# Seven-product weight tiles taken one product after another, added up by TensorE on copies of its own sums, with every low part of these tiles on VectorE and six plain column tiles in place of four

## The chip, the cores and the metric

The kernel runs on one NeuronCore of a Trainium2 chip. The metric is the device time of one execution in microseconds (us), as the median of several runs.

## What is computed

A decoder trunk of two layers for 512 tokens of width 1024: layer 0 mixes with an RWKV-7 recurrence, layer 1 with dilated attention over keys and values that were made once from the stream. Each layer has a gated FFN (SwiGLU, width 2816) ahead of its mixer and one behind it, so four FFNs in all. The change touches the FFNs alone, and each of them computes

```python
def swiglu(h, w_in, w_out):
    gate, up = jnp.split(h @ w_in, 2, axis=-1)
    return (jax.nn.silu(gate) * up) @ w_out

x = x + 0.5 * swiglu(rms_norm(x, g), w_in, w_out)   # D_MODEL = 1024, D_FF = 2816, SEQ = 512
```

## The kernel before

The five engines run written-out programs of their own and meet at semaphores; nothing is scheduled by a library. Activations lie transposed, features on the partitions and the 512 tokens along the row. To keep float32 accuracy in TensorE's float32r format, each operand is split into a high part and a low part (the difference), and each product is made of three matmuls: high by high, high by low, low by high. The high part is a copy by ScalarE (ACT, `w_hi`), the low part a subtraction of two tiles in SBUF (`w_lo<-w_raw,w_hi`).

Weights come in chunks of 128 x 1024 values through four slots (`w_raw`, `w_hi`, `w_lo`, `SLOTS = 4`). A chunk's raw slot may be loaded again when its low part is made, its split parts may be overwritten when TensorE has used it (`w_used`).

An FFN has 22 column tiles of 128 hidden features (`FT`). They go through in three stages:

- **Plain groups.** `PLAIN = 2` groups of two column tiles each, four chunks to a group, 96 matmuls of 512 columns (gate and up, eight rows of 128 features, three products' parts). Group g uses banks 0 to 3 or 4 to 7. RMSNorm's factor `rstd` is multiplied in afterwards by VectorE (DVE), L747 and L749. GpSimd (POOL) makes the low parts, L343.
- **Seven-product tiles.** `TILES = 18` column tiles, two chunks each, from the normed stream `xa`. Gate and up of both halves of the tokens (256 each) over both halves of the features form a 2 x 2 by 2 x 2 block product, done with seven products instead of eight (Winograd's form of Strassen's). A product is 12 matmuls of 256 columns, a tile is 84. Before them VectorE makes sums of the weights, `weight_sums` (L588, L590, L591, L593; three into `wt`, one in place in `w_raw`), and once for each FFN the sums of the activations `xs`. The seven products of a tile lie in seven half banks, and each k-step issues a part of all seven. When the tile is done VectorE reads them and adds (L760 to L771: eight instructions of 128 x 256, each with one operand in PSUM), ScalarE takes Silu (L682), and VectorE multiplies to `hid` (L742). ScalarE makes the high parts (`weight_his`, L607 and L608); the low parts are divided: two sums and the chunk itself on GpSimd (L614, L343), the third sum on VectorE (L599).
- **Output rows.** 22 chunks of `w_out` by `hid`, 24 matmuls of 512 columns each, all eight banks.

Seven-product tiles alternate between banks 0 to 3 and 4 to 7. On each engine the order is that of the code: `step(n)` of VectorE, for instance, makes the weight sums of a later chunk, adds up tile n, makes the sums of the next chunk and its low part. `wt` and `wt_lo` share their memory, so the sums of a chunk also wait until TensorE has used the chunk four before it.

## Time and profile before

| | |
|---|---|
| median of 3 runs | 2620.65 us (2619.97 to 2623.49) |
| the profiled execution's own time | 2614.64 us |
| its span | 2612.9 us |
| TensorE busy | 2457.2 us, 94% of the span |
| VectorE busy | 1723.5 us, 66% |
| ScalarE busy | 1037.8 us, 40% |
| GpSimd busy | 1292.9 us, 49% |
| mean granted TensorE clock | 0.98 |

Busy time of TensorE (PE) is an upper bound of its work, since matmuls overlap: a 256-column matmul's record lasts 0.28 us, while the next one starts 0.12 us after it. So gaps and start-to-start times are read here, rather than busy shares. In rows of the trace, what stands in brackets is the time that the engine was idle before the instruction and what ended that idle time.

### The profile page before, as it was taken

The page shows a single profiled execution, that of the slowest core. Times are in us where ns is not written, and L with a number is a line of the kernel's source. Part 1 is how long each engine was busy: PE and PEld are TensorE (multiplying, and loading weights), DVE is VectorE, ACT ScalarE, POOL GpSimd, SP SyncE. Part 2 cuts the span into 40 slices and gives each one's busy share as a digit, 9 for nine tenths or more (in the row PEclk, how much of TensorE's full clock was granted, in tenths as well). Part 3 has the DMA queues.
Part 4 walks back from the last instruction along what each step waited for, and adds up shares of the span by engine and source line. Part 5 has one row for each costly group of instructions (what it writes and reads, how often), then busy time and mean ns, then how long its engine had stood idle before and what let it go on. Part 6 is the DMA issues. An engine that isn't in the chain of part 4 may idle for free.

```text
span 2612.9 us, 51432 instructions
## 1 busy us (share of the span) xinstructions
PE 2457.2 (94%) x20298; PEld 2110.5 (81%) x20298; DVE 1723.5 (66%) x2510; ACT 1037.8 (40%) x1655; POOL 1292.9 (49%) x641
## 2 busy tenths in 40 slices
PE   7899999998888989999999998999999998799998
PEld 6799886767776779988888878998888777699987
DVE  7999656456663799953433169995463566799943
ACT  4333324634562433332443233343353664333332
POOL 3777544333434467754344447775443102477742
PEclk9899999998998999999999999999999999899999
DMA  4233332210002223332344433333233241133331
GB/s 130 73 96 96 114 93 85 89 45 4 5 4 66 65 81 96 96 113 97 97 145 143 139 105 89 90 95 120 95 99 97 73 130 57 49 91 94 105 106 63
DMA packets 256570, 230.76 MB, mean 88 GB/s; under 512 B 17464, under 2 KB 194776, under 8 KB 256408
## 3 DMA queue, kind: packets, MB, share of 16 engines
q1 hardware_dynamic: 256408, 228.47, 28.1%
q8 instruction: 118, 1.93, 0.3%
q14 instruction: 44, 0.36, 0.0%
HBM read 213.73 MB, written 14.68 MB: 87 GB/s over the span
## 4 chain that ended last, share of the span: by engine, by line
PE 57%; POOL 18%; issue 16%; DVE 6%; ACT 2%; DMA 0%; POOLq 0%; SPq 0%; ACTq 0%; DVEq 0%
PE bank L368 9%; PE bank L370 9%; PE bank L369 9%; POOL wt_lo L614 8%; POOL w_lo L343 8%; PE bank L375 5%; PE bank L376 5%; PE bank L377 5%; DVE xa L621 2%; PE bank L2419 1%; PE bank L2406 1%; PE bank L2441 1%; POOL xs_lo L653 1%; PE bank L1635 1%; PE bank L1593 1%
## 5 line engine op out<-in xcount | busy, mean ns | idle before, releaser
L343 POOL TENSOR_TENSOR w_lo<-w_raw,w_hi 128x1024 fp32r<-128x1024 f32 x376 | 932.8, 2486 | 871.8 <-ACT w_hi L338 864.1
L338 ACT ACTIVATE w_hi<-w_raw 128x1024 fp32r<-128x1024 f32 x232 | 242.2, 1056 | 509.5 <-PE bank L370 336.0
L614 POOL TENSOR_TENSOR wt_lo<-wt,wt_hi 128x512 fp32r<-128x512 f32 x144 | 233.0, 1618 | 227.6 <-ACT w_hi L608 227.6
L883 PE MATMUL bank<-xa_hi,w_hi 128*128 128x256 f32 x864 | 258.9, 300 | 77.2 <-DVE wt_lo L599 38.2
L673 DVE TENSOR_TENSOR hid_hl<-hid,hid_hl 128x512 fp32r<-128x512 f32 x80 | 177.0, 2216 | 213.2 <-ACT hid_hl L667 213.2
L607 ACT ACTIVATE wt_hi<-wt 128x768 fp32r<-128x768 f32 x144 | 121.8, 846 | 466.4 <-DVE wt L593 465.7
L883 PEld LDWEIGHTS bank<-xa_hi,w_hi 128*128 128x128 f32 x864 | 166.5, 193 | 103.4 <-issue 85.9
L370 PE MATMUL bank<-hid_hl,w_lo 128*128 128x512 f32 x640 | 249.0, 389 | 0.0
L368 PE MATMUL bank<-hid_hl,w_hi 128*128 128x512 f32 x640 | 249.0, 389 | 0.0
L369 PE MATMUL bank<-hid_hl,w_hi 128*128 128x512 f32 x640 | 249.0, 389 | 0.0
L884 PE MATMUL bank<-xa_lo,w_hi 128*128 128x256 f32 x864 | 245.7, 284 | 0.0
L885 PE MATMUL bank<-xa_hi,w_lo 128*128 128x256 f32 x864 | 245.3, 284 | 0.0
L375 PE MATMUL bank<-w_hi,xg_hi 128*128 128x512 f32 x576 | 226.9, 394 | 0.0
L377 PE MATMUL bank<-w_lo,xg_hi 128*128 128x512 f32 x576 | 224.4, 390 | 0.0
L376 PE MATMUL bank<-w_hi,xg_lo 128*128 128x512 f32 x576 | 224.2, 389 | 0.0
L590 DVE TENSOR_TENSOR wt<-w_raw,wt 128x256 f32<-128x256 f32 x144 | 202.8, 1408 | 5.0
L884 PEld LDWEIGHTS bank<-xa_lo,w_hi 128*128 128x128 f32 x864 | 166.9, 193 | 0.2
L885 PEld LDWEIGHTS bank<-xa_hi,w_lo 128*128 128x128 f32 x864 | 166.7, 193 | 0.0
L883 PE MATMUL bank<-xs_hi,wt_hi 128*128 128x256 f32 x576 | 164.4, 286 | 0.0
L884 PE MATMUL bank<-xs_lo,wt_hi 128*128 128x256 f32 x576 | 164.4, 285 | 0.0
L885 PE MATMUL bank<-xs_hi,wt_lo 128*128 128x256 f32 x576 | 164.2, 285 | 0.0
L608 ACT ACTIVATE w_hi<-w_raw 128x1024 fp32r<-128x1024 f32 x144 | 150.3, 1044 | 0.0
(351 smaller groups left out, 6078.7 us busy)
## 6 DMA issues: line engine op xcount, KB each, us to landing
w_raw<-in_ffn_w_in SPq DMA_DIRECT2D x352, 256.0 KB, 3.2
w_raw<-in_ffn_w_out SPq DMA_DIRECT2D x176, 256.0 KB, 2.8
w_raw<-in_w_kv SPq DMA_DIRECT2D x96, 256.0 KB, 3.1
w_raw<-in_rwkv_w_rkv SPq DMA_DIRECT2D x48, 256.0 KB, 2.9
w_raw<-in_attn_w_q SPq DMA_DIRECT2D x48, 256.0 KB, 3.0
k_dram<-stage SPq DMA_DIRECT2D x6, 1024.0 KB, 4.6
v_dram<-stage SPq DMA_DIRECT2D x6, 1024.0 KB, 5.6
keys<-k_dram SPq DMA_DIRECT2D x24, 256.0 KB, 3.7
```

What stands on the lines that cost most here:

```text
L338: act.activation(w_hi[:, s, :], w_raw[:, s, :], ACT.Copy).then_inc(w_hi_ready, 1)
L343: pool.tensor_tensor(w_lo[:, s, :], w_raw[:, s, :], w_hi[:, s, :].bitcast(F32), ALU.subtract).then_inc(w_lo_ready, 1)
L368: pe.matmul(o, hi, x_hi, start=start, stop=False)
L369: pe.matmul(o, hi, x_lo, start=False, stop=False)
L370: return pe.matmul(o, lo, x_hi, start=False, stop=stop)
L375: pe.matmul(o, x_hi, hi, start=start, stop=False)
L376: pe.matmul(o, x_lo, hi, start=False, stop=False)
L377: return pe.matmul(o, x_hi, lo, start=False, stop=stop)
L614: pool.tensor_tensor(wt_lo[:, s, 0:2], wt[:, s, 0:2], wt_hi[:, s, 0:2].bitcast(F32), ALU.subtract)
L883: pe.matmul(o, hi, x_hi, start=k == 0 and m % 2 == 0, stop=False, skip_group_check=True)
L884: pe.matmul(o, hi, x_lo, start=False, stop=False, skip_group_check=True)
L885: last = pe.matmul(o, lo, x_hi, start=False, stop=k == KP - 1, skip_group_check=True)
```

## The change

- `PLAIN = 3`: three plain groups (six column tiles) and 16 seven-product tiles in each FFN.
- A tile's seven products are issued one after another, 12 matmuls each. Four half banks hold them: `C11`, `P5`, `C21`, `C12`. Where a product has to be added to several sums, ScalarE copies the running sum from one bank to the next (`copy` in `frame`), and TensorE adds its next product onto that copy. A tile has four such copies, counted by `snapshot`; TensorE waits for the first ahead of its third product, for the second ahead of its fifth, and for all four ahead of its last one. ScalarE takes Silu straight from the banks, in two halves. Of the eight additions of VectorE two remain (`ups`).
- All low parts of the seven-product stage are VectorE's: `weight_sums_lo` subtracts 128 x 768 and 128 x 1024; the seven `normed_los` are VectorE's too. GpSimd does nothing in this stage. Two counters of chunks take the place of one (`wait_lo`).
- In the plain stage ScalarE's order changes: all four chunks 4 to 7 are split before Silu and before the high parts of the normed stream.

```diff
-        PLAIN = 2
+        PLAIN = 3
...
-        def weight_last_lo(dve, ph, q, i=None):
+        def weight_sums_lo(dve, ph, q, i=None):
...
             dve.wait_ge(w_hi_ready, plus(c + 1, i, SLOTS))
-            dve.tensor_tensor(wt_lo[:, s, 2], wt[:, s, 2], wt_hi[:, s, 2].bitcast(F32), ALU.subtract).then_inc(wt_last_ready, 1)
+            dve.tensor_tensor(wt_lo[:, s], wt[:, s], wt_hi[:, s].bitcast(F32), ALU.subtract)
+            dve.tensor_tensor(w_lo[:, s, :], w_raw[:, s, :], w_hi[:, s, :].bitcast(F32), ALU.subtract).then_inc(wt_lo_ready, 1)
...
-        def weight_los(pool, ph, q, i=None):
-            c = seven_start(ph) + q
-            s = c % SLOTS
-            pool.wait_ge(w_hi_ready, plus(c + 1, i, SLOTS))
-            pool.tensor_tensor(wt_lo[:, s, 0:2], wt[:, s, 0:2], wt_hi[:, s, 0:2].bitcast(F32), ALU.subtract)
-            split_lo(pool, c, i, SLOTS)
...
+            def copy(n, product, dst, src, i=None):
+                act.wait_ge(product_done, plus(5 * (ph["nth"] * TILES + n) + product, i, 10))
+                act.activation(dst, src, ACT.Copy).then_inc(snapshot, 1)
...
+            def frame(n, i=None):
+                his(2 * n + 2, i)
+                copy(n, P1_DONE, seven_bank(n, C21), seven_bank(n, C11), i)
...
+                    second_silu(n - 1, i)
+                his(2 * n + 3, i)
+                copy(n, P6_DONE, seven_bank(n, C12), seven_bank(n, C21), i)
+                copy(n, P5_DONE, part[:, n % 2, 0], seven_bank(n, P5), i)
+                copy(n, P7_DONE, part[:, n % 2, 1], seven_bank(n, C21), i)
...
+                act.activation(gate[:, n % 2, first], seven_bank(n, C11), ACT.Silu)
...
-            for j in range(SLOTS, 2 * SLOTS - 1):
-                split_hi(act, c0 + j)
-            normed_his(act, ph, slice(0, 4))
-            split_hi(act, c0 + 2 * SLOTS - 1)
-            for t in range(2):
-                silu(t)
-            normed_his(act, ph, slice(4, 7))
+            for j in range(SLOTS, 2 * SLOTS):
+                split_hi(act, c0 + j)
+            for t in range(2):
+                silu(t)
+            for j in range(2 * SLOTS, 2 * SLOTS + 2):
+                split_hi(act, c0 + j)
...
+            normed_his(act, ph, slice(0, 3))
+            split_hi(act, c0 + 2 * SLOTS + 2)
+            normed_his(act, ph, slice(3, 7))
+            split_hi(act, c0 + 2 * SLOTS + 3)
...
-            if ph["update"] is None:
-                for i in range(2):
-                    dve.wait_ge(stored[i], 16 * (len(KV_GROUPS) // 2))
             normed_dve(dve, ph)
-            plain(0)
-            weight_sums(dve, ph, 0)
-            normed_lo_dve(dve, ph)
-            weight_last_lo(dve, ph, 0)
+            plain_scaled(0)
+            normed_los(dve, ph, slice(A11, S2))
+            plain_times(0)
+            normed_los(dve, ph, slice(S2, S3))
+            plain_scaled(1)
+            plain_times(1)
+            weight_sums(dve, ph, 0)
             weight_sums(dve, ph, 1)
+            for q in range(2):
+                weight_sums_lo(dve, ph, q)
+            normed_los(dve, ph, slice(S3, A22 + 1))
             weight_sums(dve, ph, 2)
...
+                product(n, c11, b11, A11, start=True).then_inc(product_done, 1)
+                product(n, p5, t1, S1, start=True).then_inc(product_done, 1)
+                read(1)
+                product(n, c21, t2, S2).then_inc(product_done, 1)
+                product(n, c11, b21, A12).then_inc(product_done, 1)
+                read(2)
+                product(n, c21, t3, S3).then_inc(product_done, 1)
+                product(n, c12, b22, S4, js=(0,))
+                read(4)
+                product(n, c21, t4, A22, js=(0,)).then_inc(w_used, 1)
+                product(n, c12, b22, S4, js=(1,))
+                product(n, c21, t4, A22, js=(1,)).then_inc(w_used, 1)
```

On ScalarE, a steady seven-product tile of the first FFN stood so before (in brackets the semaphores that a row waits for; L607 and L608 are the high parts of a chunk's sums and of the chunk, L682 is Silu):

```order
L607 ACTIVATE wt_hi<-wt 128x768 [waits w_used,wt_ready]
L608 ACTIVATE w_hi<-w_raw 128x1024
L607 ACTIVATE wt_hi<-wt 128x768 [waits w_used,wt_ready]
L608 ACTIVATE w_hi<-w_raw 128x1024
L682 ACTIVATE gate<-gate 128x512 [waits gate_scaled]
```

and stands so now (L706 are the copies of sums, L710 and L726 the two halves of Silu):

```order
L631 ACTIVATE wt_hi<-wt 128x768 [waits w_used,wt_ready]
L632 ACTIVATE w_hi<-w_raw 128x1024
L706 ACTIVATE bank<-bank 128x256 [waits product_done]
L710 ACTIVATE gate<-bank 128x256 [waits w_used]
L631 ACTIVATE wt_hi<-wt 128x768 [waits w_used,wt_ready]
L632 ACTIVATE w_hi<-w_raw 128x1024
L706 ACTIVATE bank<-bank 128x256 [waits product_done]
L706 ACTIVATE part<-bank 128x256 [waits product_done] x2
L726 ACTIVATE gate<-bank 128x256
```

ScalarE's row of a tile has gained four copies and one Silu instruction, and the first copy stands behind the high parts of the next tile's first chunk.

On VectorE, the same tile stood so before (L588 to L593 are the weight sums, L599 a low part, L760 to L771 the additions):

```order
L588 TENSOR_TENSOR wt<-w_raw 128x256 [waits w_used,w_landed1_1,w_landed1_0]
L590 TENSOR_TENSOR wt<-w_raw,wt 128x256 [waits wt_step]
L591 TENSOR_TENSOR w_raw<-w_raw 128x2x128
L593 TENSOR_TENSOR wt<-w_raw,wt 128x256 [waits wt_step]
L599 TENSOR_TENSOR wt_lo<-wt,wt_hi 128x256 [waits w_hi_ready]
L760 COPY part<-bank 128x256 [waits w_used]
L762 TENSOR_TENSOR part<-bank,part 128x256 [waits sums_step]
L763 TENSOR_TENSOR gate<-bank,part 128x256
...
L771 TENSOR_TENSOR up<-bank,up 128x256 [waits sums_step]
L742 TENSOR_TENSOR hid<-gate,up 128x512 [waits up_scaled,silu_done]
```

and stands so now:

```order
L616 TENSOR_TENSOR wt<-w_raw,wt 128x256 [waits wt_step]
L798 TENSOR_TENSOR up<-bank,part 128x256 [waits w_used,snapshot]
L799 TENSOR_TENSOR up<-bank,part 128x256
L622 TENSOR_TENSOR wt_lo<-wt,wt_hi 128x768 [waits w_hi_ready]
L623 TENSOR_TENSOR w_lo<-w_raw,w_hi 128x1024
L779 TENSOR_TENSOR hid<-gate,up 128x512 [waits up_scaled,silu_done]
L622 TENSOR_TENSOR wt_lo<-wt,wt_hi 128x768 [waits w_hi_ready]
L623 TENSOR_TENSOR w_lo<-w_raw,w_hi 128x1024
L611 TENSOR_TENSOR wt<-w_raw 128x256 [waits w_used,w_landed2_1,w_landed2_0]
```

Two low parts of 768 and two of 1024 columns have come in, six additions and two low parts of 256 columns have gone.

## Rows read from the trace of the kernel before

**Rows 1.** The page: busy time of each engine, and the chain that ended last.

```profile
PE 2457.2 (94%) x20298; PEld 2110.5 (81%) x20298; DVE 1723.5 (66%) x2510; ACT 1037.8 (40%) x1655; POOL 1292.9 (49%) x641
...
PE 57%; POOL 18%; issue 16%; DVE 6%; ACT 2%; DMA 0%; POOLq 0%; SPq 0%; ACTq 0%; DVEq 0%
```

**Rows 2.** Windows: the seven-product stages of two of four FFNs; busy, clock, DMA.

```profile
922.45:1124.47 202.02, 191.72 (x1513) 184.97 (x1514) 194.10 (x335) 77.93 (x93) 148.82 (x73) 0.99 0.32 96
1571.36:1773.39 202.03, 190.83 (x1513) 185.14 (x1514) 194.06 (x335) 77.91 (x93) 148.86 (x73) 0.99 0.33 96
```

**Rows 3.** Timeline of PE, steady tile of the first FFN: start, length, instruction, idle.

```profile
153.67 0.28 PE L884 MATMUL bank<-xa_lo,w_hi 128*128 128x256 f32 x1
...
158.46 0.28 PE L885 MATMUL bank<-xa_hi,w_lo 128*128 128x256 f32 x1
159.16 0.38 PE L883 MATMUL bank<-xa_hi,w_hi 128*128 128x256 f32 x1 [0.43 <-POOL w_lo L343]
...
170.27 0.38 PE L883 MATMUL bank<-xa_hi,w_hi 128*128 128x256 f32 x1 [0.44 <-POOL w_lo L343]
```

**Rows 4.** Timeline of DVE, the next tile.

```profile
160.96 2.51 DVE L590 TENSOR_TENSOR wt<-w_raw,wt 128x256 f32<-128x256 f32 x1
...
164.40 0.41 DVE L588 TENSOR_TENSOR wt<-w_raw 128x256 f32<-128x256 f32 x1
...
165.52 0.42 DVE L593 TENSOR_TENSOR wt<-w_raw,wt 128x256 f32<-128x256 f32 x1
...
168.21 0.41 DVE L768 TENSOR_TENSOR gate<-bank,part 128x256 f32<-128x256 f32 x1
```

**Rows 5.** Timeline of ACT, the same tile.

```profile
164.25 0.85 ACT L607 ACTIVATE wt_hi<-wt 128x768 fp32r<-128x768 f32 x1 [6.04 <-DVE wt L593]
165.01 1.04 ACT L608 ACTIVATE w_hi<-w_raw 128x1024 fp32r<-128x1024 f32 x1
166.06 0.85 ACT L607 ACTIVATE wt_hi<-wt 128x768 fp32r<-128x768 f32 x1
...
168.66 0.64 ACT L682 ACTIVATE gate<-gate 128x512 f32<-128x512 f32 x1 [0.81 <-DVE gate L768]
```

**Rows 6.** Line 647 (DVE, low parts of 1024 columns): ns least/median/most, starts.

```profile
L647 DVE TENSOR_TENSOR xa_lo<-xa,xa_hi x16: 1211/1746/3355, 70.0 to 2276.2; 128x1024 fp32r<-128x1024 f32 x16
```

**Rows 7.** Timeline of PE, start of the second FFN's second group, and after.

```profile
885.02 0.50 PE L368 MATMUL bank<-xg_hi,w_hi 128*128 128x512 f32 x1 [0.34 <-POOL w_lo L343]
...
905.26 0.55 PE L368 MATMUL bank<-xg_hi,w_hi 128*128 128x512 f32 x1 [3.61 <-POOL w_lo L343]
...
922.45 0.55 PE L883 MATMUL bank<-xa_hi,w_hi 128*128 128x256 f32 x1 [9.83 <-DVE wt_lo L599]
```

**Rows 8.** Windows: after the 3.61 us gap, and an undisturbed plain group.

```profile
906.50:910.00 3.50, 3.50 (x12) 2.76 (x11) 3.47 (x3) 1.59 (x2) 3.50 (x2) 0.64 0.55 151
...
1541.60:1563.30 21.70, 21.70 (x96) 17.65 (x94) 17.13 (x16) 10.23 (x12) 10.16 (x4) 1.00 0.18 52
```

**Rows 9.** Timeline of DVE, start of the second FFN.

```profile
881.29 11.82 DVE L621 SCALAR_TENSOR_TENSOR xa<-x,par,rstd 128x512 f32<-128x512 f32 x8 [0.70 <-ACT rstd L489]
893.15 1.23 DVE L628 TENSOR_TENSOR xs<-xa 128x1024 f32<-128x1024 f32 x1
...
897.82 1.28 DVE L747 TENSOR_TENSOR gate<-bank,rstd 128x512 f32<-128x512 f32 x2
...
914.18 7.83 DVE L647 TENSOR_TENSOR xa_lo<-xa,xa_hi 128x1024 fp32r<-128x1024 f32 x4
```

**Rows 10.** Timeline of ACT, the same stretch.

```profile
901.74 1.04 ACT L338 ACTIVATE w_hi<-w_raw 128x1024 fp32r<-128x1024 f32 x1
```

**Rows 11.** Timeline of POOL, the same stretch.

```profile
882.28 8.29 POOL L343 TENSOR_TENSOR w_lo<-w_raw,w_hi 128x1024 fp32r<-128x1024 f32 x3 [7.85 <-ACT w_hi L338]
```

**Rows 12.** Timeline of PE, start of the first FFN's output rows.

```profile
283.30 0.50 PE L368 MATMUL bank<-hid_first,w_hi 128*128 128x512 f32 x1 [0.22 <-DVE up L771]
```

More of the change, by code:

```diff
@@ L310, in plus, with wait_lo @@
             return const if i is None else i * step + const
+        def wait_lo(eng, c, i=None, step=0):
+            starts = [seven_start(ph) for ph in plan if "n" in ph]
+            before = sum(min(max(c + 1 - s, 0), WT_CHUNKS) for s in starts)
+            if any(s <= c < s + WT_CHUNKS for s in starts):
+                eng.wait_ge(wt_lo_ready, plus(before, i, step))
+            else:
+                eng.wait_ge(w_lo_ready, plus(c + 1 - before, i, step))
         def load_chunk(sp, c, halves, i=None, step=0):
@@ L524, in build, with seven_bank @@
         NORMED_STEPS = KT + 4
-        SUMS_STEPS = NORMED_STEPS + 4 * TILES
+        C11, C21, C12, P5 = range(4)
+        P1_DONE, P5_DONE, P6_DONE, P2_DONE, P7_DONE = range(1, 6)
+        first, second = slice(0, HT), slice(HT, T)
+        def seven_bank(n, m):
+            return bank[4 * ((n + PLAIN) % 2) + m][:, 0:HT]
         def hid_at(f):
@@ new lines, in ups, with seven_times @@
+            def ups(n, i=None):
+                f = n % 2
+                dve.wait_ge(snapshot, plus(4 * (ph["nth"] * TILES + n + 1), i, 8))
+                dve.wait_ge(w_used, plus(cs + 2 * n + 2, i, SLOTS))
+                dve.tensor_tensor(up[:, f, first], seven_bank(n, C12), part[:, f, 0], ALU.add)
+                dve.tensor_tensor(up[:, f, second], seven_bank(n, P5), part[:, f, 1], ALU.add).then_inc(up_scaled, 1)
+            def seven_times(n, i=None):
+                t = 2 * PLAIN + n
@@ L822, in ffn_pool @@
                 split_lo(pool, c)
[L823 to L826 removed]
             c1 = out_start(ph)
+            wait_lo(pool, c1 - 1)
             split_lo_run(pool, c1, min(FT + LEAD, CHUNKS - c1))
@@ L857, in group, with product @@
                     last.then_inc(w_used, 1)
-            def seven(n, i=None):
-                b = 4 * (n % 2)
-                first, second = slice(0, HT), slice(HT, T)
-                for j in range(2):
-                    c, at = cs + 2 * n + j, ph["nth"] * WT_CHUNKS + 2 * n + j
-                    s = c % SLOTS
-                    pe.wait_ge(w_lo_ready, plus(c + 1, i, SLOTS))
-                    pe.wait_ge(wt_last_ready, plus(at + 1, i, SLOTS))
-                    if j == 0:
-                        if n == 0:
-                            pe.wait_ge(normed_lo_ready, 7 * (ph["nth"] + 1))
-                        pe.wait_ge(up_scaled, base + 2 if n == 0 else plus(base + n + 3, i, 2))
+            def product(n, o, weight, name, js=(0, 1), start=False):
+                if n == 0:
+                    pe.wait_ge(normed_lo_ready, 7 * ph["nth"] + name + 1)
+                for j in js:
+                    c = cs + 2 * n + j
+                    s = c % SLOTS
@@ L879, in seven @@
-                        a11, a12, s3, a22 = [(xa_hi[:, k, o, ts], xa_lo[:, k, o, ts]) for ts in (first, second) for o in range(2)]
-                        for m, ((hi, lo), (x_hi, x_lo)) in enumerate((
-                                (b11, a11), (b21, a12), (b22, s4), (t4, a22), (t1, s1), (t2, s2), (t3, s3))):
-                            o = bank[b + m // 2][:, m % 2 * HT:(m % 2 + 1) * HT]
-                            pe.matmul(o, hi, x_hi, start=k == 0 and m % 2 == 0, stop=False, skip_group_check=True)
-                            pe.matmul(o, hi, x_lo, start=False, stop=False, skip_group_check=True)
-                            last = pe.matmul(o, lo, x_hi, start=False, stop=k == KP - 1, skip_group_check=True)
@@ L886, in seven @@
-                    last.then_inc(w_used, 1)
+                        hi, lo = weight(s, e)
+                        x_hi, x_lo = [normed_places(*t)[name][:, k] for t in ((xa_hi, xs_hi), (xa_lo, xs_lo))]
+                        pe.matmul(o, hi, x_hi, start=start and k == 0, stop=False, skip_group_check=True)
+                        pe.matmul(o, hi, x_lo, start=False, stop=False, skip_group_check=True)
+                        last = pe.matmul(o, lo, x_hi, start=False, stop=k == KP - 1, skip_group_check=True)
@@ L891, in ffn_pe @@
                 pe.wait_ge(v_odd, 2 * KEYS_GROUPS)
-            group(c0 + G_CHUNKS, 1, 1)
+            for g in range(1, PLAIN):
+                group(c0 + g * G_CHUNKS, g, g % 2)
             for n in range(2):
```

214 lines of the change are left out of this document (109 added, 105 removed).

## Prediction

> **What bounds it now.** I read the page first: TensorE is busy 94% of the span, and in the chain that ended last GpSimd holds 18% [rows 1]. That is a lot for an engine that can't be the bound by its busy time, so somewhere TensorE waits for its low parts. Windows over the FFNs show where to look: the seven-product stage takes 202.0 us in each FFN for 18 tiles, 11.22 us a tile [rows 2]. Inside a steady tile two matmuls 40 places apart start 153.67 and 158.46, so a matmul takes 0.1198 us and 84 of them 10.06 us [rows 3]. Tiles start 11.11 us apart, at 159.16 and 170.27, each behind a gap that ended with GpSimd's low part [rows 3]. So a steady tile loses about 1.0 us.
>
> The timeline of VectorE says why it can't be early: a 128 x 256 subtraction from SBUF takes 2.51 us while GpSimd works and 0.41 when it doesn't [rows 4]. The two hold each other up: weight sums wait for GpSimd, ScalarE waits for the sums, GpSimd for ScalarE.
>
> The stage's start costs more. In the second FFN TensorE waits 3.61 us inside group 1, for a chunk whose high part stands behind the normed stream on ScalarE, at 901.74 [rows 7, 10], and 9.83 us ahead of the first seven-product tile [rows 7]. After such a gap the clock is granted at 0.64 in the mean of the next 3.5 us (part of it at 1.2 GHz), which loses 3.5 x 0.36 = 1.3 us [rows 8].
>
> **The change part by part.** TensorE first, pure work. From the start of group 1 (885.02) to the end of the stage (1124.47) it now takes 239.45 us [rows 2, 7]. A plain group takes 21.7 [rows 8]. New: two groups, 43.4, and 16 tiles of 10.06, 161.0; together 204.4 us. The two tiles that become plain cost 1.6 us more than as seven-product tiles, which is in this sum.
>
> VectorE in a steady tile: without GpSimd the four sums of a chunk take 1.54 us (164.40 to 165.94 [rows 4]), 0.385 each at 256 columns; four instructions of 1024 columns take 4.67 (893.15 to 897.82 [rows 9]), 1.17 each, in line with the least length of 1.21 [rows 6]; 768 columns lie between, at 0.91. Eight sums 3.1, low parts 2 x (0.91 + 1.17) = 4.2, two additions 0.8, one product of 512 columns 0.64 (half of 1.28 [rows 9]): 8.7 us of 10.06. It isn't the bound while GpSimd is silent; if the low parts took their contended 1.75 us [rows 6] it would be (8.7 + 2 x 0.6 = 9.9, plus waits).
>
> ScalarE in a tile: high parts 2 x 1.81 (164.25 to 166.06 [rows 5]), four copies and two half Silus. No row shows a 256-column copy between banks. ScalarE's lengths of 0.64, 0.85 and 1.04 at 512, 768 and 1024 columns [rows 5] leave 0.42 at 256; bounds are 0.3 and 0.64 (the 512-column row). Sum 6.0 us, so ScalarE isn't the bound either. What counts is when a copy is done.
>
> Two chains of handovers decide that. A handover takes 0.04 (VectorE's end 168.62 to Silu 168.66) to 0.12 us (165.94 to 164.25 plus a tile's 1.81, that is 166.06) [rows 4, 5].
> First chain: the first chunk of a tile is given back with matmul 72 of 84, which ends 1.28 us before the tile's end; VectorE's sums take 1.54; then ScalarE's two high parts, 0.76 + 1.05; then the copy, 0.42. With three or four handovers it lands 2.6 to 3.0 us into the next tile. The third product's weights would load at 24 x 0.12 - 0.12 = 2.76. Late by 0 to 0.2.
> Second chain: the fifth product ends at 7.36, its copy is done 0.42 later, 7.86 to 8.0 with handovers; the half product placed as cover ends so that the next load is due at 7.80. Late by 0.06 to 0.2.
> I take 0.2 us a tile from both, a tile of 10.26 us; bounds 0.0 and 0.7 (a copy of 0.64).
> The Trainium skill, "VectorE: DVE Perf Modes", section on the TRN2 errata, gives ScalarE reading PSUM 172 cycles plus one an element, an estimate of 0.36 us a copy; no row shows this form. By it each chain is 0.06 shorter and the whole comes out 8 us lower, about 2518.
>
> Start of the stage, second FFN. Chunk 7 is now split right after chunk 6, so the 3.61 us gap goes; GpSimd has four low parts in a row at 2.76 (8.29 / 3 [rows 11]), to 893.3, which keeps VectorE's eight `xa` instructions (11.82 us beside three [rows 9]) 2 us longer. Then the sums of `xs` (893.15 to 897.82, 4.7 us) and the first scaling, 2 x 1.2: VectorE at 902.3. ScalarE: two Silus, two splits, three high parts of about 1 us: the first low part can start at 905.5. Low parts of GpSimd lie beside the next four VectorE items (about 2 us each, as in 7.83 / 4 [rows 9]), to 915.5. From there GpSimd is silent: two low parts 2.3, scaling 2.4, products 1.2, sums of two chunks 2.9, a wait for ScalarE 0.7, their low parts 4.0, three low parts 3.4, sums of the third chunk 1.5: 934. ScalarE splits that (1.9) and only then copies the first product: 936.5. TensorE ends group 2 at 885.0 + 43.4 = 928.4 and wants this copy 2.9 us later, at 931.3. It waits about 5.2 us. Two whole Silus (1.1) and another chunk's high parts (1.8) stand between this copy and the second one, which costs 1.1 more. With 0.5 for a late first low part, the first tile loses 6.8 us, and the clock after such a gap 1.3 [rows 8].
> So the stage ends at 928.4 + 10.06 + 6.8 + 1.3 + 15 x 10.26 = 1100.5 instead of 1124.47: 24.0 us less. The first and fourth FFN have the same start, with gaps of the same size.
> Third FFN: there group 1 runs without a gap and ends at 1563.3 [rows 8]; the stage begins 8.1 us later, at 1571.36 [rows 2]. VectorE no longer waits for stores before `xa`, and the new group 2 ends at 1585.0, by which time the chunks' sums are ready (VectorE starts there earlier, and from group 2 on only follows TensorE's giving back of slots). I give 0.5 us: 1585.0 + 10.06 + 0.5 + 153.9 = 1749.5 against 1773.39, 23.9 less.
> At the end of the stage TensorE now waits for the last product `hid` rather than for `up`; four banks' worth of matmuls (12 x 0.226 = 2.7 us) lie before that wait, against Silu, two additions and a product that has a GpSimd low part beside it (up to 2.9 us). It waited 0.22 us there [rows 12]; I put the difference at nothing, 0 to 1 us an FFN.
> DMA: each chunk's load starts when its slot's low part is made, over ten us ahead of use; nothing there.
>
> **Sum.** 3 x 24.0 + 23.9 = 96 us off 2614.64 gives 2519 for an execution like the profiled one. That one was 6.0 below the median of the runs, so the forecast is 2525 us.
>
> **Rivals.**
> - *Late copies.* ScalarE's copy takes 0.64, or several waits add up behind the high parts. Then both chains are late, 0.5 to 0.7 us a tile: 64 x 0.4 = 26 more, 2551. For it: both chains end within 0.2 us of when they are due. Against: 512 columns would have to cost what 256 do.
> - *A longer start.* VectorE's row of some 50 us before the first tile is worked out from shared stretches. 3 us more in four FFNs, with a second spell of low clock: 2525 + 12 + 5 = 2542. In the other direction, VectorE catching up during group 2 would take the 5 us wait away: 2505.
> - *The clock.* TensorE gets up to three short waits in each tile. If these made the clock fall, a tile would take 10.06 / c. The change turns into a loss where the mean c is below 0.86 (10.06 / 0.86 = 11.7, that is 96 / 64 = 1.5 over 10.26). At 0.75 a tile costs 3.35 more: 2740. Against: the stage of before has a gap in every tile [rows 3] and was granted 0.99 in the mean [rows 2]. The Trainium skill, "TensorE: Matmul & The Clock Gate", section on psum-queue depth-cycling, tells of a kernel whose small idle times between banks made the clock swing; by that rule this rival happens, and the trace of before doesn't bear it out.
> - *VectorE becomes the bound.* The change only moves GpSimd's work, and if low parts of 1024 columns didn't fall to 1.21 us, a tile would be 10.6 to 11: 2555 to 2575. Against: least lengths in rows 4 and 6.
>
> **Numbers.** A run tells 0.2% (5 us) from no change. Chances: forecast 0.60, late copies 0.17, start 0.12, VectorE bound 0.05, clock or another loss 0.06. The likeliest case alone spans 2512 to 2538; the range reaches to both start cases and late copies: 2503 to 2556. Faster 0.94, same 0.01, slower 0.05.
>
> **What would show it.** Right: tiles of the steady stretch 10.1 to 10.4 us apart; no 2.5 us weight sum on VectorE there; waits of TensorE put down to ScalarE's bank copies, a few tenths each; one wait of about 5 us in the first tile of three FFNs, none of 10; no 3.6 us gap in group 1. Wrong: tile waits for `w_lo` of VectorE (VectorE bound), copies of 0.6 us, a granted clock under 0.95 in the stage.

## The result, and the profile after

The changed kernel takes 2502.28 us (median of four runs, 2494.73 to 2508.27) against 2620.31 for the kernel before on the same chip: a ratio of 0.955, with a 95% interval of 0.9519 to 0.958. It is 118.0 us faster; the forecast was 2525 (2503 to 2556). So the direction and most of the mechanism came out, and the time fell 0.7 us outside the range, on the fast side.

The page of the changed kernel, as in [rows 1]:

```profile
PE 2430.0 (97%) x20010; PEld 2096.0 (84%) x20010; DVE 1499.2 (60%) x2138; ACT 1100.6 (44%) x1959; POOL 719.1 (29%) x357
...
PE 89%; DVE 7%; ACT 2%; issue 2%; POOL 0%; DMA 0%; SPq 0%; ACTq 0%; DVEq 0%
```

GpSimd has gone from the chain that ended last (it held 18%), and TensorE holds 89% of it. Windows over two seven-product stages, the second FFN's and the third's, which answer to [rows 2] (length; busy time and instructions of PE, PEld, DVE, ACT and POOL; granted clock, DMA share, GB/s):

```profile
902.61:1069.92 167.31, 163.48 (x1346) 163.18 (x1346) 131.83 (x236) 87.08 (x162) 4.94 (x3) 0.99 0.36 106
1530.30:1692.16 161.86, 161.86 (x1346) 161.75 (x1345) 127.05 (x229) 86.93 (x162) 4.94 (x3) 1.00 0.35 104
```

In the third FFN 16 tiles take 161.86 us, 10.12 each, with TensorE busy throughout. The steady tile, on TensorE's timeline: it starts at 989.01, the next one at 999.10, and the one matmul inside that is not 0.12 us ahead of the next is the first of the last product, at 996.93.

```profile
989.01 0.28 PE L906 MATMUL bank<-xa_hi,w_hi 128*128 128x256 f32 x1
...
996.93 0.30 PE L906 MATMUL bank<-xa_hi,wt_hi 128*128 128x256 f32 x1
997.07 0.28 PE L907 MATMUL bank<-xa_lo,wt_hi 128*128 128x256 f32 x1
...
999.10 0.28 PE L906 MATMUL bank<-xa_hi,w_hi 128*128 128x256 f32 x1
```

So a tile takes 10.09 us, where [rows 3] had 11.11. ScalarE in the same tile (the two high parts, the first copy, and after some rows the last copy):

```profile
989.54 0.85 ACT L631 ACTIVATE wt_hi<-wt 128x768 fp32r<-128x768 f32 x1 [2.56 <-DVE wt L616]
990.29 1.04 ACT L632 ACTIVATE w_hi<-w_raw 128x1024 fp32r<-128x1024 f32 x1
991.24 0.37 ACT L706 ACTIVATE bank<-bank 128x256 f32<-128x256 f32 x1
...
996.41 0.39 ACT L706 ACTIVATE part<-bank 128x256 f32<-128x256 f32 x1 [2.22 <-PE bank L908]
```

The first copy ends at 991.61, 2.60 us into the tile, where the third product's weights load at 2.76. The last one ends at 996.80, 7.79 us in, where the load is due at 7.80 and starts at 7.84:

```profile
996.85 0.19 PEld L906 LDWEIGHTS bank<-xa_hi,wt_hi 128*128 128x128 f32 x1
```

So only this last copy delays TensorE, by 0.03 to 0.04 us. And VectorE, which waits 1.68 us for TensorE in this tile and has no sum longer than 0.43:

```profile
997.86 0.43 DVE L611 TENSOR_TENSOR wt<-w_raw 128x256 f32<-128x256 f32 x1 [1.68 <-PE bank L908]
```

The start of the stage in the second FFN. VectorE (`xa`; the two products of group 0 beside GpSimd; the first sum of the third chunk), ScalarE (high part of the third chunk, first copy) and TensorE (the only wait there):

```profile
855.15 13.97 DVE L637 SCALAR_TENSOR_TENSOR xa<-x,par,rstd 128x512 f32<-128x512 f32 x8 [0.70 <-ACT rstd L498]
...
883.57 5.70 DVE L779 TENSOR_TENSOR hid<-gate,up 128x512 f32<-128x512 f32 x2
...
905.88 0.42 DVE L611 TENSOR_TENSOR wt<-w_raw 128x256 f32<-128x256 f32 x1
```

```profile
907.46 0.84 ACT L631 ACTIVATE wt_hi<-wt 128x768 fp32r<-128x768 f32 x1 [7.35 <-DVE wt L616]
...
909.16 0.37 ACT L706 ACTIVATE bank<-bank 128x256 f32<-128x256 f32 x1
```

```profile
905.47 0.28 PE L908 MATMUL bank<-xs_hi,wt_lo 128*128 128x256 f32 x1
909.58 0.58 PE L906 MATMUL bank<-xs_hi,wt_hi 128*128 128x256 f32 x1 [3.83 <-ACT bank L706]
```

The wait of [rows 7] inside group 1 and the 9.83 us ahead of the first tile are gone. One wait is left, 4.1 us from the start of one matmul to the start of the next, in the first tile of three FFNs. The clock granted after it is the third number from the end, 0.57:

```profile
909.60:913.10 3.50, 3.50 (x18) 3.50 (x19) 3.50 (x5) 3.40 (x6) 0.00 (x0) 0.57 0.00 0
```

That is the 1.2 GHz level for most of the window. The first tile takes 15.67, 15.60, 10.16 and 16.67 us in the four FFNs; the third has no such wait.

To compare the starts of stages in different runs I take one window, from the start of group 1 to the end of the seven-product stage, in the second FFN. Before and now:

```profile
885.02:1124.47 239.45, 215.71 (x1609) 204.00 (x1610) 226.97 (x360) 89.85 (x106) 169.12 (x81) 0.97 0.30 90
```

```profile
858.88:1069.92 211.04, 207.21 (x1537) 199.14 (x1538) 172.68 (x274) 105.59 (x183) 24.85 (x10) 0.99 0.35 105
```

It is 28.4 us shorter. Over the four FFNs it is 28.5, 28.4, 26.6 and 27.5, together 111.0 us of the 118.0.

### The profile page after: what moved, and what is told of

It is laid out like the page before. It is cut to its first block, busy times and chain, and to the rows that moved or that the text cites. A ratio compares the mean times of both kernels' runs of the same rounds, so it can differ in the third digit from the quotient of the medians.

```text
span 2506.5 us, 50199 instructions
## 1 busy us (share of the span) xinstructions
PE 2430.0 (97%) x20010; PEld 2096.0 (84%) x20010; DVE 1499.2 (60%) x2138; ACT 1100.6 (44%) x1959; POOL 719.1 (29%) x357
## 4 chain that ended last, share of the span: by engine, by line
PE 89%; DVE 7%; ACT 2%; issue 2%; POOL 0%; DMA 0%; SPq 0%; ACTq 0%; DVEq 0%
PE bank L377 11%; PE bank L379 10%; PE bank L378 10%; PE bank L906 9%; PE bank L907 9%; PE bank L908 9%; PE bank L384 6%; PE bank L386 6%; PE bank L385 6%; PE bank L2474 1%; PE bank L2461 1%; PE bank L2496 1%; PE bank L1690 1%; DVE hid L779 1%; PE bank L1648 1%
## 5 line engine op out<-in xcount | busy, mean ns | idle before, releaser
L352 POOL TENSOR_TENSOR w_lo<-w_raw,w_hi 128x1024 fp32r<-128x1024 f32 x248 | 614.7, 2486 | 1573.5 <-ACT w_hi L347 1562.3
L347 ACT ACTIVATE w_hi<-w_raw 128x1024 fp32r<-128x1024 f32 x248 | 259.5, 1057 | 518.1 <-PE bank L379 357.4
L906 PE MATMUL bank<-xa_hi,w_hi 128*128 128x256 f32 x768 | 218.6, 285 | 0.0
L907 PE MATMUL bank<-xa_lo,w_hi 128*128 128x256 f32 x768 | 218.0, 284 | 0.0
L908 PE MATMUL bank<-xa_hi,w_lo 128*128 128x256 f32 x768 | 217.9, 284 | 0.0
L623 DVE TENSOR_TENSOR w_lo<-w_raw,w_hi 128x1024 fp32r<-128x1024 f32 x128 | 156.4, 1222 | 0.0
L377 PE MATMUL bank<-xg_hi,w_hi 128*128 128x512 f32 x384 | 152.0, 396 | 3.6 <-issue 2.5
L378 PE MATMUL bank<-xg_lo,w_hi 128*128 128x512 f32 x384 | 150.2, 391 | 0.0
L379 PE MATMUL bank<-xg_hi,w_lo 128*128 128x512 f32 x384 | 150.0, 391 | 0.0
L907 PEld LDWEIGHTS bank<-xa_lo,w_hi 128*128 128x128 f32 x768 | 148.3, 193 | 0.0
```

The source lines that it names most:

```text
L347: act.activation(w_hi[:, s, :], w_raw[:, s, :], ACT.Copy).then_inc(w_hi_ready, 1)
L352: pool.tensor_tensor(w_lo[:, s, :], w_raw[:, s, :], w_hi[:, s, :].bitcast(F32), ALU.subtract).then_inc(w_lo_ready, 1)
L377: pe.matmul(o, hi, x_hi, start=start, stop=False)
L378: pe.matmul(o, hi, x_lo, start=False, stop=False)
L379: return pe.matmul(o, lo, x_hi, start=False, stop=stop)
L906: pe.matmul(o, hi, x_hi, start=start and k == 0, stop=False, skip_group_check=True)
```

## The experiments

All edits are made to the changed kernel. "Window" is the one just shown, 211.04 us in the changed kernel; its edges are read to 0.05 us. The kernel before ran beside each run, on the same chip. The runs with one more copy and with the normed high parts first ran on the chip of "changed kernel, again"; the others ran on three more chips, so for them the ratios are the closer comparison.

| run | median us | ratio to before, 95% interval | window us |
|---|---|---|---|
| changed kernel, again | 2503.38 | 0.9553 (0.9528 to 0.9579) | 211.05 |
| two plain groups | 2522.87 | 0.9624 (0.9595 to 0.9653) | 218.54 |
| chunk's low part on GpSimd | 2546.66 | 0.9708 (0.9675 to 0.9742) | 221.66 |
| ScalarE's old order | 2496.94 | 0.9525 (0.9503 to 0.9548) | 210.51 |
| copies first at the start | 2497.35 | 0.9529 (0.9506 to 0.9552) | 209.88 |
| one more copy, first chain | 2510.63 | 0.9573 (0.9548 to 0.9599) | 212.72 |
| one more copy, last chain | 2518.20 | 0.9609 (0.9581 to 0.9637) | 216.33 |
| normed high parts first | 2497.52 | 0.9524 (0.9497 to 0.9552) | 209.95 |
| both start orders | 2499.24 | 0.9547 (0.9524 to 0.9569) | 210.50 |
| four plain groups | 2494.88 | 0.9531 (0.9518 to 0.9544) | 207.40 |
| group 2's low parts on VectorE | 2487.73 | 0.9501 (0.9482 to 0.9521) | 205.83 |

**The changed kernel, once more.**

> The changed kernel itself, unaltered, once more beside the others: what a second profile of it shows. Theory: the first tile's wait of 4.1 us in three FFNs, tiles of 10.09 us and stages of 167.2 us come back to 0.1 us, and the time within 0.3% of 2502; the difference between one execution and the median lies outside the FFNs' stages. Rival: the wait or the tile varies between executions.

Tiles of 10.09, waits of 4.11 us in three first tiles, 2503.38 us. The stage of the second FFN comes back (167.37 against 167.31). The first FFN's does not come back to 0.1 us: its first tile takes 16.84 instead of 15.67, behind the same wait, so it is the clock's part that varies. In sum the four windows take 839.4 us in the first profile and 840.2 in this one, while all that lies outside them takes 1667.1 and 1657.6. So nearly all of what differs between the two executions lies outside. The same instructions between the first FFN's stage and the second FFN's group 1, first in the changed kernel's first profile, then in this one:

```profile
254.00:858.90 604.90, 570.41 (x8515) 454.05 (x8513) 336.23 (x480) 260.43 (x489) 237.67 (x152) 0.96 0.17 54
```

```profile
253.80:852.70 598.90, 566.30 (x8515) 449.93 (x8514) 338.09 (x480) 259.76 (x489) 237.24 (x152) 0.97 0.18 54
```

6 us on the same instructions of the same kernel, with the granted clock at 0.96 and 0.97. The profiled executions' own times are 2508.27 and 2499.57.

**Is it the tiles or the third plain group?** Undone: `PLAIN = 3`, and with it that group's splits, its scaling and products on VectorE, and the order in which the output rows begin.

```diff
-        PLAIN = 3
+        PLAIN = 2
...
```

> The new tiles, copies and low parts on VectorE with two plain groups instead of three, 18 seven-product tiles. The third plain group is 1.5 us dearer for TensorE than the two tiles it replaces (21.7 against 2 x 10.09). Theory: its use is to cover VectorE's row ahead of the first tile. In the changed kernel the first copy lands at 909.5 in the second FFN and is due at 905.4. Without the group it is due 21.7 us sooner, at 883.8, while VectorE's row loses only one scaling and one pair of products (3.7 us) and the contention of up to four low parts (about 3 us): it lands at about 902.5. The wait ahead of and in the first tile is then about 18.7 us instead of 4.1 in three FFNs: 3 x 14.6 less 4 x 1.5, with up to 5 us in the third FFN, is 38 to 43 us more than the changed kernel's 2502, about 2543; tiles stay at 10.09. Rival: the waits at the start hang on ScalarE's and VectorE's order alone, and the group gives no cover: 6 us less than the changed kernel, 2496.

2522.87: 97 of the 118 us are there without the third group, which is worth some 20 us, half of the 38 to 43 that were expected, although it costs TensorE 1.5 us in each FFN. The mechanism is the expected one, waits ahead of the first tile and in it, but of 9.5 and 2.7 us (12.2 together), not 18.7:

```profile
891.50 0.58 PE L900 MATMUL bank<-xa_hi,w_hi 128*128 128x256 f32 x1 [9.13 <-DVE w_lo L623]
898.47 0.58 PE L900 MATMUL bank<-xs_hi,wt_hi 128*128 128x256 f32 x1 [2.44 <-ACT bank L706]
```

The third product of the first tile starts 38.2 us after group 1 (860.3), against 50.7 in the changed kernel: 12.5 us sooner, where 6.7 were expected. VectorE's row of instructions ahead of the first tile is shorter by more than the 3.7 us of work taken out. That pointed to GpSimd's four low parts, which in the changed kernel lie beside this row, and to the last experiment below.

**Is it GpSimd that made the old tiles slow?**

```diff
             dve.tensor_tensor(wt_lo[:, s], wt[:, s], wt_hi[:, s].bitcast(F32), ALU.subtract)
-            dve.tensor_tensor(w_lo[:, s, :], w_raw[:, s, :], w_hi[:, s, :].bitcast(F32), ALU.subtract).then_inc(wt_lo_ready, 1)
...
+                pool.tensor_tensor(w_lo[:, s, :], w_raw[:, s, :], w_hi[:, s, :].bitcast(F32), ALU.subtract).then_inc(wt_lo_ready, 1)
...
```

> The low part of each seven-product chunk's own weights (1024 columns) goes back to GpSimd, after VectorE has made the low part of the sums; all else as in the changed kernel. VectorE has 2.3 us less to do in a tile, GpSimd 4.8 to 5.5 us. Theory: what slowed the old tiles is that VectorE's two-input operations from SBUF stall beside GpSimd. VectorE then loses 2.1 us for each GpSimd operation that it meets (2.51 against 0.41), so a tile costs 0.3 to 1.0 us more: 64 x 0.3 to 1.0 = 19 to 64 us, 2521 to 2566, and sums of 2.5 us stand on VectorE again. Rival: the old loss came from the order of the products and the sums made on VectorE, not from GpSimd; VectorE has slack of 1.7 us a tile, so tiles stay at 10.1 and the time within 5 us of 2502.

2546.66, 43 us more, in the range of the theory, though VectorE has less to do. Tiles take 10.65 us. VectorE and GpSimd in one of them:

```profile
1003.88 2.51 DVE L622 TENSOR_TENSOR wt_lo<-wt,wt_hi 128x768 fp32r<-128x768 f32 x1 [0.57 <-ACT w_hi L631]
1008.00 1.23 DVE L611 TENSOR_TENSOR wt<-w_raw 128x256 f32<-128x256 f32 x1 [1.61 <-PE bank L917]
1009.27 0.43 DVE L613 TENSOR_TENSOR wt<-w_raw,wt 128x256 f32<-128x256 f32 x1
```

```profile
1002.87 2.70 POOL L868 TENSOR_TENSOR w_lo<-w_raw,w_hi 128x1024 fp32r<-128x1024 f32 x1 [4.59 <-DVE wt_lo L622]
1006.55 2.40 POOL L868 TENSOR_TENSOR w_lo<-w_raw,w_hi 128x1024 fp32r<-128x1024 f32 x1 [0.98 <-DVE wt_lo L622]
```

The sum that starts at 1008.00, alone 0.43 us long, ends at 1009.23, 0.28 after GpSimd's instruction (1008.95). It stands at the head of the first chain, which has 0.16 us of slack, so 0.8 more there makes about the 0.56 us a tile. (36 of the 43 us; the rest are waits for GpSimd ahead of the first two tiles.) The 768-column low part takes 2.51 instead of 0.95 and costs nothing, since VectorE waits for TensorE behind it. The Trainium skill, "SBUF — State Buffer", section "Who interferes with whom", says that a VectorE instruction with two SBUF inputs and a GpSimd one that reads SBUF share a port, which the first one holds to its end. The trace agrees: the stalled sum ends just behind GpSimd's instruction. The old tile was 1.02 us longer than the new one (11.11 against 10.09), and this one GpSimd instruction for each chunk brings 0.56 of it back. How the rest divides between GpSimd's other low part and the old order of products and additions, no run shows.

**How late are the copies?** ScalarE makes one more copy of the same product, to a scratch (`square`), ahead of the first copy, or (with `P7_DONE`, in every tile but the last of a stage) ahead of the last.

```diff
                 act.wait_ge(product_done, plus(5 * (ph["nth"] * TILES + n) + product, i, 10))
+                if product == P1_DONE:
+                    act.activation(square[:, n % 2, first], src, ACT.Copy)
...
```

> In every tile ScalarE makes one more 128 x 256 copy of the first product (from PSUM to a scratch in SBUF) right ahead of the first copy. Theory: the first copy lands 0.16 us before TensorE would load the third product's weights, so 0.30 us more on ScalarE (the spacing of two such copies) makes TensorE late by 0.14 to 0.2 in each steady tile: tiles of 10.23 to 10.3 us instead of 10.09, 64 x 0.17 = 11 us more than the changed kernel, about 2513. Rival: this chain has more slack than the trace's modelled ends tell, nothing moves: 10.09 and 2502. Rival 2: the forecast's late copies: the chain was late already, and all of the 0.3 counts: 10.4 and 2521.

> In every tile but the last of a stage ScalarE makes one more 128 x 256 copy of the fifth product (to a scratch) right ahead of the last copy. Theory: the last copy lands 0.01 us before the load that needs it, so all of 0.30 counts: tiles of 10.37 to 10.41 us, 60 x 0.3 = 18 us more than the changed kernel, about 2520. Rival: hidden, 2502.

Windows over the third FFN's stage, which took 161.86 in the changed kernel, with the extra first copy and with the extra last copy:

```profile
1531.13:1694.26 163.13, 162.97 (x1346) 162.23 (x1345) 127.04 (x229) 90.44 (x178) 4.93 (x3) 1.00 0.35 103
```

```profile
1537.93:1703.73 165.80, 165.31 (x1346) 162.25 (x1345) 127.05 (x229) 91.00 (x177) 4.93 (x3) 1.00 0.34 101
```

The first chain gives tiles of 10.12 and 10.23 in turn, 0.08 more in the mean, and 2510.63: 7 us more than the changed kernel beside it, where 11 were expected. The last chain gives 10.37, 0.28 more for 0.28 of copy, and 2518.20: 15 more, where 18 were expected. So one chain had 0.2 us of slack in the mean and the other none, and a later copy does cost what the forecast thought; the copies are just not late.

**What is ScalarE's new order worth?** The last chunk of group 1 is split behind the first three normed high parts again.

```diff
-            for j in range(SLOTS, 2 * SLOTS):
+            for j in range(SLOTS, 2 * SLOTS - 1):
                 split_hi(act, c0 + j)
+            normed_his(act, ph, slice(0, 3))
+            split_hi(act, c0 + 2 * SLOTS - 1)
...
-            normed_his(act, ph, slice(0, 3))
...
```

> ScalarE splits the last chunk of group 1 behind the three first normed high parts again, ahead of the two Silus, as the kernel before did; all else as in the changed kernel. That chunk is needed at about 875.1 in the second FFN and would be ready at 880.7: a wait of about 5.5 us inside group 1 in three FFNs. Theory: what follows (VectorE's row of low parts, sums and scalings) doesn't wait for TensorE there, so the first tile's wait of 4.1 us shrinks to nothing and the stage ends only 1.4 to 2 us later in each of three FFNs, with a clock spell moved but not added: 4 to 8 us more than the changed kernel, about 2508. Rival, as the forecast had it (the gap counts in full): 5.5 x 3 = 16 us more, with an added clock spell of 1.3 each 20: 2518 to 2522.

Neither the 4 to 8 us more of the theory nor the 16 to 20 of the rival came out: 2496.94, not above the changed kernel (the intervals overlap). The gap is back inside group 1, and the first tile has no wait at all (10.14 us):

```profile
874.51 0.50 PE L377 MATMUL bank<-xg_hi,w_hi 128*128 128x512 f32 x1 [3.18 <-POOL w_lo L352]
```

```profile
854.70:1065.21 210.51, 207.31 (x1537) 198.84 (x1538) 170.89 (x274) 105.66 (x183) 25.25 (x10) 0.99 0.36 105
```

The gap is 3.57 us and the wait that it replaces 4.11. Not splitting the last chunk early also spares VectorE one GpSimd instruction beside `xa`: 11.81 us instead of 13.97. VectorE is now ready sooner and waits for TensorE, which stood in its own gap and so gives back a weight slot later:

```profile
892.88 0.43 DVE L611 TENSOR_TENSOR wt<-w_raw 128x256 f32<-128x256 f32 x1 [3.34 <-PE bank L379]
```

So it isn't VectorE's row that sets the start here; the time is lost in the gap itself. One more thing shows here: in the first FFN the clock stayed at full speed behind this gap, in the second and the fourth it fell to 1.2 GHz.

**Copies first at the start.** The first copy ahead of the third chunk's high parts, the next two ahead of the two whole Silus.

```diff
+                if n > 0:
+                    his(2 * n + 2, i)
                 copy(n, P1_DONE, seven_bank(n, C21), seven_bank(n, C11), i)
                 if n == 0:
+                    his(2)
+                    copy(0, P6_DONE, seven_bank(0, C12), seven_bank(0, C21))
+                    copy(0, P5_DONE, part[:, 0, 0], seven_bank(0, P5))
...
```

> In the first tile of each stage ScalarE takes the first copy ahead of the high parts of chunk 2, and the second and third copy ahead of the two plain Silus; all else as in the changed kernel. Theory: the wait of 4.1 us in the first tile is ScalarE's order, not a lack of data: the copy's input is there at 904.1, and the copy is made at 909.2 only because it stands behind the high parts. With it gone the next wait is tile 1's for its low parts, made by VectorE until 916.5, against 918.3 when that tile starts now. The stage ends 1.8 us sooner in three FFNs, and 1 us more where the low clock after the gap goes: 5 to 9 us less, 2493 to 2497. Rival 1: the forecast's view that VectorE's row sets the first tile: no change beyond 1 us an FFN. Rival 2: nothing else waits, 3 x 4.1 + 4 = 16 us less, 2486.

2497.35, at the upper end of the theory in time, but the intervals overlap with the changed kernel's and the window is only 1.2 us shorter. One wait has become four short ones, the third of them for VectorE:

```profile
898.46 0.38 PE L911 MATMUL bank<-xa_hi,w_hi 128*128 128x256 f32 x1 [0.95 <-ACT bank L706]
901.75 0.39 PE L911 MATMUL bank<-xa_hi,wt_hi 128*128 128x256 f32 x1 [0.87 <-ACT part L706]
905.44 0.39 PE L911 MATMUL bank<-xa_hi,w_hi 128*128 128x256 f32 x1 [1.27 <-DVE w_lo L623]
...
909.00 0.39 PE L911 MATMUL bank<-xs_hi,wt_hi 128*128 128x256 f32 x1 [0.42 <-ACT bank L706]
```

Tile 1, the second tile, starts at 905.44, 57.6 us after group 1 (847.8), which is when VectorE's row of 57.6 us ends in the changed kernel too (916.5 less 858.88). Here the row sets the start: it has no wait for TensorE in it, and TensorE waits for its last low part. No low clock followed these waits.

**Normed high parts first, and both orders together.**

```diff
+            normed_his(act, ph, slice(0, 3))
             for t in range(2):
                 silu(t)
             for j in range(2 * SLOTS, 2 * SLOTS + 2):
                 split_hi(act, c0 + j)
...
-            normed_his(act, ph, slice(0, 3))
```

> ScalarE makes the first three normed high parts right when VectorE's sums of xs are there, ahead of the two Silus and the splits of two chunks, and still splits the last chunk of group 1 early; all else as in the changed kernel. Theory: VectorE's row ahead of the first tile stood idle 2.35 us for these high parts, and the first copy hangs on the end of that row; the row ends about 2 us sooner, the first tile waits 2.1 us instead of 4.1 in three FFNs and group 1 keeps no gap: 6 us less than the changed kernel, 2496, up to 10 less if the low clock after the wait goes too. Rival: VectorE only meets more of GpSimd's low parts in the time won, as it does in the run with the old order of ScalarE: nothing is won, 2502.

2497.52, 1.5 us above the theory's 2496 and not on its path. The first tile has no wait (10.1 us), and a wait of 3.0 us stands at the start of group 2 instead, for the chunk that is now split behind the high parts. VectorE's idle time of 2.35 us became 1.88, and further on it waits 2.51 us for a slot from TensorE:

```profile
888.51 0.42 DVE L611 TENSOR_TENSOR wt<-w_raw 128x256 f32<-128x256 f32 x1 [2.51 <-PE bank L379]
```

> Both edits of ScalarE's order at the start: the three normed high parts ahead of the Silus and two splits, and the copies of the first tile ahead of high parts and Silus. Theory: each alone reached the end of VectorE's row (tile 1 starts 57.6 to 58.9 us after group 1's start, against 59.4 in the changed kernel), so together they win at most 0.7 us an FFN more: 2495 to 2498, a wait of 3.0 us left at the start of group 2. Rival: the gains add, 2491 to 2492.

2499.24, a little above the theory's 2495 to 2498: nothing added, as it said. With the 3.0 us wait left, the other copy order only makes the first two tiles 10.47 each. Five orders of ScalarE, the changed kernel's among them, give windows of 209.9 to 211.0 us, and it would be easy to conclude that one cause sets them all. The rows above say otherwise. In the changed kernel and with the copies first, TensorE waits at the end of VectorE's row. In the other three a gap of 3.0 or 3.57 us stands ahead of that, and VectorE waits 2.5 to 3.3 us for TensorE. Each of those three orders brings VectorE to its first weight sums sooner (33.3 to 33.6 us after group 1's start, against 36.2) and pays about as much in the gap.

**Four plain groups.**

```diff
-        PLAIN = 3
+        PLAIN = 4
...
```

> Four plain groups and 14 seven-product tiles; the three last normed low parts, the sums of the first two chunks and their low parts come behind the products of the third plain group on VectorE, and group 3's chunks are split by ScalarE behind group 2's; tiles as in the changed kernel. Theory: what sets the first two tiles is VectorE's row, which ends 57.6 us after the start of group 1 in the changed kernel whatever ScalarE's order; a fourth group makes tile 1 due 21.7 us later, so no wait is left in the first tile and no low clock. A group costs 1.5 us more than the two tiles: 3 x (5.5 to 6.7 less 1.5) less 1.5 for the third FFN is 10 to 14 us less than the changed kernel, 2489 to 2493. Rival: four more low parts on GpSimd beside VectorE's row (8 us of it in the run with two groups) push it out by as much as the group gives, and a gap comes up at a plain group: no gain, 2502 to 2510.

2494.88, 8.5 less than the changed kernel's second median and 0.0022 in the ratio, which is 6 us; the intervals of the ratios still touch, and 10 to 14 were expected. The waits in the first tiles are gone but for 0.17 us in the second FFN (10.15, 10.49, 10.14, 10.16). The window shown is 3.6 us shorter, where 4.0 to 5.2 were expected; the four windows together are 11.1 us shorter (828.2 against 839.4). The three last normed low parts take 3.42 each beside GpSimd's new ones, which cost nothing here: VectorE waits 3.54 us for TensorE behind them.

**Less contention in VectorE's row.** VectorE makes the low parts of group 2's four chunks itself; GpSimd stops ahead of that group.

```diff
...
+            for c in range(c0 + 8, c0 + 10):
+                chunk_lo(c)
             normed_los(dve, ph, slice(A11, S2))
             plain_times(0)
             normed_los(dve, ph, slice(S2, S3))
+            for c in range(c0 + 10, c0 + 12):
+                chunk_lo(c)
...
```

> The low parts of group 2's four chunks (1024 columns each) are made by VectorE instead of GpSimd, two behind the first scaling and two ahead of the second; all else as in the changed kernel. Theory: beside GpSimd's low parts VectorE's row ahead of the first tile runs long (two products take 5.70 us where alone 1.28, a normed low part 3.43 where alone 1.21), so a low part on GpSimd costs VectorE over 2 us and made by VectorE itself 1.13. The row ends 4 us sooner, 53 us after group 1's start; tile 1 is due at 54.2, so no wait is left in the first tile and no low clock, and group 1 keeps no gap: 5 to 6 us an FFN less in three FFNs, 15 to 18 us less than the changed kernel, 2486 to 2489, and below the kernel with four plain groups. Rival: VectorE's row only grows by the four low parts (4.5 us) and the first tile waits 8 us: 2512 to 2516.

2487.73, the fastest of all, where the theory put it: 15.6 less than the changed kernel's second median, 0.0052 in the ratio, which is 14 us, and the only run whose interval lies wholly below that of the changed kernel's second set (it overlaps the first set's, which starts at 0.9519). Its slowest run (2490.62) is faster than the fastest of the changed kernel's ten (2494.73). The four windows together are 16.6 us shorter. More work on the engine whose row sets the start makes the row shorter. VectorE now (two low parts of chunks, a normed one, two products that took 5.70 before), and the window:

```profile
864.87 2.36 DVE L831 TENSOR_TENSOR w_lo<-w_raw,w_hi 128x1024 fp32r<-128x1024 f32 x2 [0.46 <-ACT w_hi L347]
867.14 1.22 DVE L667 TENSOR_TENSOR xa_lo<-xa,xa_hi 128x1024 fp32r<-128x1024 f32 x1
...
869.41 1.28 DVE L779 TENSOR_TENSOR hid<-gate,up 128x512 f32<-128x512 f32 x2
```

```profile
847.00:1052.83 205.83, 205.78 (x1537) 197.85 (x1538) 170.09 (x278) 105.39 (x183) 13.28 (x6) 1.00 0.36 107
```

The first copy starts 46.2 us after group 1 instead of 50.3, TensorE is busy for all but 0.05 of 205.83 us, and the granted clock is 1.00. VectorE has no wait for TensorE in this row, so it is the row itself that got shorter.

## Why the prediction was right, and where it was off

*Pure work.* A tile was put at 10.06 and takes 10.09; group 1 and 2 were put at 43.4 and take 43.7. Right.

*The steady tile.* The mechanism was right: two chains of handovers decide, VectorE and ScalarE are no bound, no 2.5 us sum is left, GpSimd is silent. The step that failed is the term "I take 0.2 us a tile from both", the lateness of the two chains. It measured 0.03. The ranges worked out for the chains were 2.6 to 3.0 and 7.86 to 8.0; the copies landed at 2.60 and 7.79. The bounds of the term reached down to 0.0, so the forecast had what happened as its lower edge, and took more than that. The copy was taken as 0.42 and takes 0.37 (0.38 to SBUF), and the handovers lie at the short end of theirs. 60 steady tiles by 0.17 is 10 us, the largest part of the 22.7 us between the forecast and the median. The sign that was to show it right, waits of TensorE for the copies of a few tenths in each tile, did not come. The Trainium skill's figure, quoted in the forecast from "VectorE: DVE Perf Modes", section on the TRN2 errata, gave 0.36 a copy and 8 us less; the trace is near it, with 0.37 from bank to bank and 0.38 to SBUF. The rival *late copies* did not happen, but it was a fair risk: in the runs with one more copy, 0.28 us more of ScalarE cost 0.08 us a tile in the first chain and 0.28 in the last.

*The start.* The forecast had the first copy end at 936.5 less 885.0, 51.5 us after group 1. It starts at 50.3 and ends at 50.7. This is the second term that was mis-sized: of the 8.1 us put on a first tile (5.2 and 1.1 of waits, 0.5 for the first low part, 1.3 of clock) it lost 5.6, 5.5 and 6.6, by one wait of 4.1 and the clock. The second copy and the first low part cost no wait of their own. That is about 2.2 us less in each of three FFNs, 6.6 us in all. The working also has a slip in it: four items of about 2 us behind 905.5 end at 913.5, not 915.5. It came out near all the same, by luck, because these items took 10.6 us (878.65 to 889.27), beside GpSimd more than 2 us each. `xa` beside four low parts was right (13.97 against 11.82, as said 2 us longer). The third FFN's first tile took 10.16, where 10.56 were put.

*"The 3.61 us gap goes."* It goes, and the run with ScalarE's old order shows that this by itself wins nothing: with the gap of 3.57 us back, the wait in the first tile is gone. With the chunk split early, `xa` takes 13.97 us instead of 11.81, VectorE comes to its first weight sums 36.2 us after group 1's start instead of 33.3, and the first tile pays for it. The forecast had the 2 us on `xa` in its row, but took the gap as a gain of its own.

*The sum.* Profile against profile the four windows gained 111.0 us, where 96 were forecast: 10.2 from the tiles and 6.6 from the first tiles, less about 2 in small terms. Taken off the median of before, 111.0 gives 2509.3, so about 7 us more lie outside the windows, where the forecast had nothing. That is the range of one kernel's own executions: what lies outside the windows took 1662.6 us in the profiled execution of before, and 1667.1 and 1657.6 in the two of the changed kernel, 6 of these 9.5 us in one stretch between two FFNs at another granted clock. So no profile shows a gain outside, and where the 7 us come from stays open. Without them the time would have been inside the range: that it fell just outside hangs on them as much as on the two terms.

*The other rivals.* *The clock*: it stayed at 1.00 in the third FFN's stage. The changed kernel's tiles there lose only 0.03 us each, so they hardly test this rival; the run with low parts on GpSimd does, with waits of 0.3 to 0.4 us in nearly every tile, and its stage there was granted 1.00 too. *VectorE becomes the bound*: it waits 1.7 us a tile, so it isn't. *A longer start*: it was neither longer nor was the wait gone, as the other direction of this rival had it; 4.1 of the 5.2 us were left. End of the stage: no wait of TensorE there.

## What to carry to other kernels

- When a wait moves under every reordering and the window around it stays within 1.2 us (five orders here), look at whether the engine that is waited for is itself idle. In two of the five VectorE's row was the bound; in the other three VectorE waited up to 3.3 us for TensorE, and the loss was a gap elsewhere. What helped in the end was to shorten the long row, or to put cover ahead of its end; two plain groups, three and four show what cover is worth.
- Price a low part on GpSimd by what VectorE loses beside it. Here four of them, moved to VectorE at 1.2 us each, gave the window 5.2 us back, the low clock included. A two-input instruction at the head of a chain with little slack is best kept clear of GpSimd: at 0.16 us of slack, 0.80 us of stall made a tile 0.56 longer.
- A chain that is due within 0.1 us of its end is as likely on time as late: give it its own range, from nothing up, rather than the middle of the estimates.

## What the runs showed of the hardware

- A 128 x 256 ScalarE copy from bank to bank takes 0.37 us, and the next instruction starts about 0.1 us ahead of its recorded end (two such copies start 0.28 apart). TensorE then adds onto the copy without extra time that shows: a tile of 84 matmuls takes 10.09 us, where 84 times the 0.1198 us between matmuls is 10.06.
- The drop of the clock is not certain. In the seven profiles with three plain groups and a single wait of 3.0 to 4.4 us (start to start) in three FFNs, it fell to 1.2 GHz behind 20 of the 21 waits; the exception is one of the three gaps of 3.57 us. What it costs varies too: the first tile behind the same wait of 4.11 us took 15.6 to 16.8 us in the changed kernel's two profiles. Behind waits of 0.95, 0.87, 1.27 and 0.42 us in the first two tiles it never fell, in three FFNs of one profile.
